# One step of a convolution / latent attention backbone: a new order for the opening, a layer norm in parts, masks built later

## The chip, the core and the metric

The kernel runs on one core of one Trainium2 chip. The core has a matrix engine (TensorE, PE in the rows), a vector engine (VectorE, DVE), a scalar engine (ScalarE, ACT), a general one (GpSimd, POOL) and SyncE (SP), which here only issues transfers. Each has its own strictly ordered queue; they meet in semaphores. The metric is the time of one execution on the device in microseconds. Everything is float32. Where a product must be exact and fast, each operand is kept as a high and a low part (`fp32r`), and three matmuls, high x high, high x low and low x high, make one product (`mm3`). Some products are left as plain f32 matmuls; each of these is two records in the trace.

## The reference, cut to what matters

```python
def adaln(cond, w, b):
    m = jax.nn.silu(cond) @ w + b                    # w: 1024 x 6144
    return jnp.split(m[:, None, :], N_MOD, axis=-1)  # shift1, scale1, gate1, shift2, scale2, gate2

hp = modulate(rms_norm(xp, norm1_g[i]), mp[0], mp[1])   # 128 context tokens
hs = modulate(rms_norm(xs, norm1_g[i]), ms[0], ms[1])   # 256 latent tokens

def conv_module(h, pw1, dw, dw_b, ln_g, ln_b, pw2):
    a, g = jnp.split(h @ pw1, 2, axis=-1)            # pw1: 1024 x 2048
    u = a * jax.nn.sigmoid(g)
    u = depthwise_conv(u, dw, width=31) + dw_b
    u = jax.nn.silu(layer_norm(u, ln_g, ln_b))
    return u @ pw2
```

Layer 0 is this module and a dense SwiGLU, layer 1 latent attention and a mixture of eight experts, of which each token takes two. There are two condition vectors (`c` and `c_ctx`), so the modulation product has two rows.

## The kernel before

Weights come in chunks of 1 MB (128 partitions x 2048 floats) into a ring `raw` of six slots. SyncE's queue is one written list of `load` calls: slot s is loaded when chunk s - 6 has been used (modulation) or split into its two parts (all else). `make_hi` (ScalarE, 1.9 us) and `make_lo` (VectorE, 2.3 us) split a chunk into `wh` and `wl`, rings of three.

Opening (layer 0). Chunks 0 to 7 are `ada_w`, columns 0 to 2047 (shift and scale), 128 input channels each; x comes after the third. `ada` multiplies one: four matmuls of 512 columns, column block j to PSUM partitions 32j and up:

```python
for j in range(4):
    last = pe.matmul(ps[32 * j:32 * j + 32, ADA_BANKS[q][0], :], cst[:, k, :], raw[:, s % RAW, j * 512:(j + 1) * 512], ...)
```

All eight have to be in before `add_bias`, `turn_rows` (transposes) and `modulation` give shift and scale for each channel. `norm_act` then modulates the eight transposed blocks of 128 channels, `split_block` splits them, and eight rounds r of the first projection follow: chunk `PW1 + 3r` holds 256 output channels for all 1024 input channels, 48 matmuls of 384 tokens each, and after them two modulation chunks of group 1 (`ada`). After each second round comes the sigmoid (`sig`), and `glu(t)` writes `u`. VectorE puts the taps of six of the eight channel blocks between its other work (`add_taps`, `ROUND_TAPS`, `POST_TAPS`). TensorE does the last two blocks as 62 matmuls with diagonal matrices, which ScalarE makes, with twelve modulation chunks between them.

Layer norm. The column sums and squares are summed on TensorE over all partitions; one square root and one reciprocal over all 399 columns, then eight blocks: scale (VectorE), SiLU (ScalarE), split (VectorE), and `pw2_block` for each.

Experts (layer 1). The first tile's rows are gathered by a matmul while six indirect transfers of GpSimd scatter all rows to `xs_dram`. After them GpSimd builds the masks `selL` of the last tile with some twenty small operations. In TensorE's list its three transposes and three narrow matmuls (`last_tile`) stand after the second chunk of the first tile's second weight. SyncE waits for the scatters before it loads `xrow` and the next tile's chunks.

## Time and profile before

| what | value |
|---|---|
| time, median of 3 runs | 1447.17 us (1446.88 to 1450.38) |
| the profiled execution's own time | 1447.64 us |
| its span | 1445.9 us |
| TensorE busy | 1369.8 us (95%) |
| VectorE busy | 1060.7 us (73%) |
| ScalarE busy | 756.3 us (52%) |
| GpSimd busy | 100.6 us (7%) |
| HBM traffic | 242 GB/s over the span |

Busy times overlap, so they don't add up to the span. The clock of TensorE has two levels, 1.2 and 2.4 GHz; a view shows it as the granted share, 0.50 or 1.00. A record's length includes the way through the array, so records that follow each other closely are longer than the distance between their starts.

### The profile page before, as it was taken

Reading aid. Unit: us, or ns where it says so; the run is one execution under the profiler, and the core shown is the slowest. Engines: PE = TensorE matmul, PEld = TensorE weight load, DVE = VectorE, ACT = ScalarE, POOL = GpSimd, SP = SyncE. Lnnn points to the kernel's source line nnn. Section 1 sums busy time; section 2 is a strip of 40 time slices with the busy share of each in tenths; the row PEclk is TensorE's granted clock in tenths of the full one; section 3 lists DMA queues with packets and bytes.
Section 4 is the critical chain, followed back from the end, with each engine's and each line's share of the span. In section 5 each row is a group of like instructions: output and inputs, shape, how many; then the busy total and the mean of one; then the engine's idle time right before and its main releaser. Section 6 shows DMA issues by size and latency. Waiting matters only on the chain.

```text
span 1445.9 us, 18716 instructions
## 1 busy us (share of the span) xinstructions
PE 1369.8 (95%) x6687; PEld 1100.4 (76%) x6687; DVE 1060.7 (73%) x1328; ACT 756.3 (52%) x764; POOL 100.6 (7%) x129
## 2 busy tenths in 40 slices
PE   4999989999999989899999978799999999999997
PEld 1885456999999978677777757587878878878875
DVE  1689985443433457888888889588888888888986
ACT  2431355222312255655555545577777777777773
POOL 2000000401000001100000015200000000000003
PEclk8999999999999989999999998899999999999999
DMA  9898556989743324322222235799999999999994
GB/s 376 293 339 322 204 203 225 400 337 64 198 145 103 122 50 128 104 66 66 79 80 87 89 116 206 301 375 375 363 385 380 364 363 395 369 362 381 385 361 152
DMA packets 91914, 351.17 MB, mean 243 GB/s; under 512 B 7279, under 2 KB 43447, under 8 KB 62679
## 3 DMA queue, kind: packets, MB, share of 16 engines
q1 hardware_dynamic: 81088, 316.95, 61.4%
q0 software_dynamic: 9040, 28.66, 5.8%
q10 hardware_dynamic: 1735, 4.89, 0.8%
q8 instruction: 30, 0.49, 0.1%
q14 instruction: 21, 0.17, 0.0%
HBM read 326.13 MB, written 24.35 MB: 242 GB/s over the span
## 4 chain that ended last, share of the span: by engine, by line
PE 81%; DVE 8%; ACT 3%; issue 3%; POOL 2%; DMA 1%; ACTq 0%; DVEq 0%
PE ps L277 23%; PE ps L279 22%; PE ps L278 22%; PE ps L1699 3%; PE ps L1644 3%; DVE wl L261 2%; DVE hm L1551 2%; PE ps L1945 2%; DMA raw<-in_conv_pw 1%; PE ps L1976 1%; ACT wh L255 1%; PE ps L1949 1%; POOL xs_dram L660 1%; PE ps L2107 1%; ACT QB L850 0%
## 5 line engine op out<-in xcount | busy, mean ns | idle before, releaser
L261 DVE TENSOR_TENSOR wl<-raw,wh 128x2048 fp32r<-128x2048 f32 x253 | 575.9, 2290 | 151.8 <-ACT wh L255 151.6
L255 ACT ACTIVATE wh<-raw 128x2048 fp32r<-128x2048 f32 x253 | 484.1, 1917 | 306.0 <-PE ps L279 267.4
L277 PE MATMUL ps<-wh,xgh 128*128 128x512 f32 x432 | 173.5, 402 | 0.1
L279 PE MATMUL ps<-wh,xgl 128*128 128x512 f32 x432 | 171.1, 396 | 0.0
L278 PE MATMUL ps<-wl,xgh 128*128 128x512 f32 x432 | 171.0, 396 | 0.0
L277 PE MATMUL ps<-hTh,wh 128*128 128x384 f32 x480 | 164.7, 343 | 1.8 <-DVE hTl L417 1.8
L278 PE MATMUL ps<-hTl,wh 128*128 128x384 f32 x480 | 163.3, 340 | 0.0
L279 PE MATMUL ps<-hTh,wl 128*128 128x384 f32 x480 | 163.0, 340 | 0.0
L277 PE MATMUL ps<-wh,hgh 128*128 128x512 f32 x288 | 118.2, 410 | 3.6 <-DVE hgl L1557 1.9
L278 PE MATMUL ps<-wl,hgh 128*128 128x512 f32 x288 | 115.8, 402 | 0.0
L279 PE MATMUL ps<-wh,hgl 128*128 128x512 f32 x288 | 115.6, 402 | 0.0
L1072 DVE SCALAR_TENSOR_TENSOR v<-u,dwT,v 128x399 f32<-128x399 f32 x180 | 99.1, 639 | 0.0
L277 PEld LDWEIGHTS ps<-hTh,wh 128*128 128x128 f32 x480 | 90.5, 189 | 10.8 <-issue 7.9
L1158 DVE TENSOR_TENSOR ff<-ps,fs 128x384 f32<-128x384 f32 x22 | 12.3, 558 | 114.9 <-PE ps L279 114.9
L279 PEld LDWEIGHTS ps<-wh,xgl 128*128 128x128 f32 x432 | 81.4, 188 | 19.8
L277 PEld LDWEIGHTS ps<-wh,xgh 128*128 128x128 f32 x432 | 81.4, 188 | 19.1 <-DVE wl L261 0.4
L278 PEld LDWEIGHTS ps<-wl,xgh 128*128 128x128 f32 x432 | 81.4, 188 | 18.3
L278 PEld LDWEIGHTS ps<-hTl,wh 128*128 128x128 f32 x480 | 90.7, 189 | 0.4
L279 PEld LDWEIGHTS ps<-hTh,wl 128*128 128x128 f32 x480 | 90.6, 189 | 0.0
L277 PEld LDWEIGHTS ps<-wh,hgh 128*128 128x128 f32 x288 | 55.2, 192 | 20.8 <-DVE wl L261 5.5
L279 PEld LDWEIGHTS ps<-wh,hgl 128*128 128x128 f32 x288 | 55.3, 192 | 13.6
L278 PEld LDWEIGHTS ps<-wl,hgh 128*128 128x128 f32 x288 | 55.4, 192 | 12.5
(368 smaller groups left out, 2122.7 us busy)
## 6 DMA issues: line engine op xcount, KB each, us to landing
raw<-in_moe_w SPq DMA_DIRECT2D x180, 1024.0 KB, 6.1
raw<-in_ada_w SPq DMA_DIRECT2D x48, 1024.0 KB, 6.6
raw<-in_ffn_w SPq DMA_DIRECT2D x33, 1024.0 KB, 11.5
raw<-in_conv_pw SPq DMA_DIRECT2D x12, 1024.0 KB, 9.2
raw<-in_mla_wo SPq DMA_DIRECT2D x8, 1024.0 KB, 4.8
xs_dram<-hf POOLq DMA_DIRECT2D x14, 512.0 KB, 21.2
ys_dram<-hf POOLq DMA_DIRECT2D x14, 512.0 KB, 22.3
raw<-in_mla_wuq SPq DMA_DIRECT2D x8, 768.0 KB, 4.6
```

The costliest lines, as they stand in the source:

```text
L255: act.activation(wh[:, split_no(s) % HL, :], raw[:, s % RAW, :], ACT.Copy).then_inc(hi_made, 1)
L261: eng.tensor_tensor(wl[:, split_no(s) % HL, :], raw[:, s % RAW, :], wh[:, split_no(s) % HL, :], ALU.subtract).then_inc(lo_made, 1)
L277: nc.tensor.matmul(out_, sh, mh, start=start, stop=False)
L278: nc.tensor.matmul(out_, sh, ml, start=False, stop=False)
L279: return nc.tensor.matmul(out_, sl, mh, start=False, stop=stop)
L660: pool.indirect_dma_start(out=xs_dram[:, :], out_offset=bass.IndirectOffsetOnAxis(ap=rows_of[:, c, i:i + 1], axis=0), in_=xn[:, c, :], in_ ...
L1072: dve.scalar_tensor_tensor(out=v[:, j, :], in0=u[:, j, w:w + CV], scalar=dwT[:, w * DK + j:w * DK + j + 1], in1=v[:, j, :], op0=ALU.mult, ...
L1551: dve.tensor_tensor(hm[:, g, :].rearrange("p (j r) -> p r j", j=4), ps[:, 3 + g, :].rearrange("p (r j) -> p r j", j=4), ms[:, g, :].rearra ...
L1644: last = pe.matmul(ps[32 * j:32 * j + 32, ADA_BANKS[q][0], :], cst[:, k, :], raw[:, s % RAW, j * 512:(j + 1) * 512], start=k == 0, stop=k ...
L1699: pe.matmul(ps[:, i, 0:CV], diag[:, m % DIAGS, :], u[:, DVE_BLOCKS + i, w:w + CV], start=w == 0, stop=w == CW - 1).then_inc(sem("diag_used ...
L1945: pe.matmul(ps[:, 2 * h + c // 2, a:b], QB[:, h, c * P:(c + 1) * P], KT[:, h, k0:k1], start=True, stop=False)
L1949: last = pe.matmul(ps[:, 2 * h + c // 2, a:b], QB[r0:r1, 2, c * P:(c + 1) * P], KR[r0:r1, k0:k1], start=False, stop=True)
```

## The change

- Opening: `ada_w` and the first half of `conv_pw1`'s columns come in other chunks. A modulation chunk holds the shift and scale columns of two channel blocks (2 x 256) for four of the eight input blocks, so two chunks (`OPEN`) give a pair p of channel blocks its modulation. Each chunk is two transfers of 512 KB. x is first in the queue. `ada_pair(p)` sums eight matmuls of 512 columns into PSUM partitions 32p to 32p + 31. Each pair has its own bias, transposes and modulation.
- The first two rounds of the projection become one pass: `open_block(k)` adds input block k to four output blocks (12 matmuls), between the pairs. Rounds 2 to 7 stay, with the sixteen chunks of group 1 as `ADA_ROUND` says.
- The taps in the rounds are 78 instead of 74 (`ROUND_TAPS`); `u` is cleared by GpSimd after the bias loads; VectorE clears `ar`.
- Layer norm: root and reciprocal in three parts (`LN_PARTS`), the first block scaled, passed through SiLU, split and waited for in these parts.
- Masks: TensorE's, ScalarE's and VectorE's steps of `last_tile` move from the first expert's tile into the static tile behind it.
- Semaphores are merged (`first_turned` into `x_turned`, `weights_made` into `tab_ready`), and the counts shift.

```diff
     ADA_G = DK
-    PW1 = ADA_G
-    ADA1 = PW1 + 3 * DK
+    QUARTERS = DK // 2
+    PAIR_BLOCKS = 4
+    OPEN = (0, 1, 3, 4, 5, 6, 8, 9)
+    ADA_ROUND = (0, 0, 3, 3, 3, 3, 2, 2)
+    PW1 = [2, 7] + [10 + r - 2 + sum(ADA_ROUND[:r]) for r in range(2, DK)]
+    ADA1 = 4 * ADA_G
     GATE1 = ADA1 + ADA_G
     PW2 = GATE1 + ADA_G
     GATE2 = PW2 + DK // 2 + 2
...
-    ROUND_TAPS = (0, 0, 13, 13, 12, 12, 12, 12)
+    ROUND_TAPS = (0, 0, 14, 14, 13, 13, 12, 12)
     POST_TAPS = (24, 30, 38)
     GATE_EARLY = 4
+    LN_PARTS = ((0, P, 0), (P, SV + P, P), (SV + P, CV, 2 * P))
     TILE_CH = 6 * NG
     NEXT = MOE + 12
...
+        def landed(s):
+
+            return 16 * (s // RAW + 1 + sum(o % RAW == s % RAW for o in range(min(s + 1, PW1[2]))))
 
...
-                make_hi(act, PW1)
-            act.wait_ge(sem("mods"), 8 * layer + 4 * n + 4)
             for j in blocks:
+                if j in (0, 4):
+                    make_hi(act, PW1[j // 4])
+                act.wait_ge(sem("mods"), 4 * (j // 2 + 1))
                 act.wait_ge(*of_norm(q, "turned", DK, j + 1))
                 for cond, a, b in ((1, 0, P), (0, P, T)):
...
-            for n in range(ADA_G):
-                if n == 3:
-                    sp.dma_start(x[:, 0, :], d["x_prompt"][0]).then_inc(sem("x_in"), 16)
-                    sp.dma_start(x[:, 1:3, :], d["x_sample"][0].rearrange("(c p) n -> p c n", p=P)).then_inc(sem("x_in"), 16)
-                load_ada(n, 0, n)
-            for r in range(DK):
-                load(sp, PW1 + 3 * r, rows(d["conv_pw1"][0], 0, DK, r % 2 * D + r // 2 * 256, 256), as_rows(256, DK))
-                for i in range(2):
-                    load_ada(PW1 + 3 * r + 1 + i, 0, ADA_G + 2 * r + i)
+            def load_pair(s, w, half, c0):
+
+                for t in range(2):
+                    load(sp, s, rows(w, 4 * half, 4, t * D + c0, 256),
+                         lambda slot: slot.rearrange("p (k t n) -> p k t n", k=4, t=2)[:, :, t, :])
+
+            sp.dma_start(x[:, 0, :], d["x_prompt"][0]).then_inc(sem("x_in"), 16)
+            sp.dma_start(x[:, 1:3, :], d["x_sample"][0].rearrange("(c p) n -> p c n", p=P)).then_inc(sem("x_in"), 16)
+            for p in range(QUARTERS):
+                for half in range(2):
+                    load_pair(OPEN[2 * p + half], d["ada_w"][0, :, 0:CH], half, 256 * p)
+                if p % 2 == 0:
+                    load_pair(PW1[p // 2], d["conv_pw1"][0], p // 2, 0)
+            n = ADA_G
+            for r in range(2, DK):
+                load(sp, PW1[r], rows(d["conv_pw1"][0], 0, DK, r % 2 * D + r // 2 * 256, 256), as_rows(256, DK))
+                for i in range(ADA_ROUND[r]):
+                    load_ada(PW1[r] + 1 + i, 0, n)
+                    n += 1
+
             def load_pw2(q):
                 load(sp, pw2_chunk(q), rows(d["conv_pw2"][0], 2 * q, 2, 0, D), as_rows(D, 2))
...
-            fetch_bias(0)
+            b = d["ada_b"][0, 0:CH].rearrange("(t q n) -> q t n", t=2, q=QUARTERS)
+            for p in range(QUARTERS):
+                pool.dma_start(ab[32 * p:32 * p + 2, 0, :].rearrange("p (t n) -> p t n", t=2),
+                               b[p].partition_broadcast(2)).then_inc(sem("bias_in0"), 16)
+            fetch_bias(0, 1)
+            pool.memset(u[:, :, :], 0.0).then_inc(sem("zeroed"), 1)
...
-            for r in range(DK):
+            for r in range(1, DK):
                 if r + 1 < DK:
-                    make_hi(act, PW1 + 3 * (r + 1))
-                for n in range(3 * r, 3 * r + 3):
-                    diagonal(n)
+                    make_hi(act, PW1[r + 1])
+                if r >= 2:
+                    for n in range(4 * (r - 2), 4 * (r - 1)):
+                        diagonal(n)
                 if r % 2 == 1:
                     t = r // 2
-                    act.wait_ge(chunk_used, used(PW1 + 3 * r))
+                    act.wait_ge(chunk_used, used(PW1[r]))
...
-            act.activation(sd, ps[:, 5, 0:CV], ACT.Sqrt, scale=1.0 / D, bias=epsc[:, 0:1]).then_inc(sem("ln_root"), 1)
-            for j in range(DK):
-                act.wait_ge(sem("ln_scaled"), j + 1)
+            for a, b, _ in LN_PARTS:
+                act.activation(sd[:, a:b], ps[:, 5, a:b], ACT.Sqrt, scale=1.0 / D, bias=epsc[:, 0:1]).then_inc(sem("ln_root"), 1)
+            for i, (_, b, o) in enumerate(LN_PARTS):
+                act.wait_ge(sem("ln_scaled"), i + 1)
+                act.activation(hf[:, 0, o:o + P], v[:, 0, b - P:b], ACT.Silu, scale=vT[:, LNG:LNG + 1],
+                               bias=vT[:, LNB:LNB + 1]).then_inc(sem("ln_done"), 1)
+            for j in range(1, DK):
+                act.wait_ge(sem("ln_scaled"), TC + j)
                 for a, b, o in ((0, P, 0), (P, T, SV - P)):
                     act.activation(hf[:, j, a:b], v[:, j, a + o:b + o], ACT.Silu, scale=vT[:, LNG + j:LNG + j + 1],
...
                 make_hi(act, MOE + k + 3)
-                if k == UP + 1:
-                    act.wait_ge(sem("last_tile"), TC + 1)
-                    for c in range(TC):
-                        act.activation(sel[:, c, :], ident[:, :], ACT.Copy, scale=rt[:, 9, c, 3:4])
...
+                    if static and k == UP + 2:
+                        act.wait_ge(sem("last_tile"), TC + 1)
+                        for c in range(TC):
+                            act.activation(sel[:, c, :], ident[:, :], ACT.Copy, scale=rt[:, 9, c, 3:4])
+                        act.activation(selT[:, :], ps[:, 6, 0:T], ACT.Copy).then_inc(sem("last_tile"), 1)
...
+            def add_bias_pair(p):
+
+                dve.wait_ge(ada_used, 2 * (p + 1))
+                if p == 0:
+                    dve.wait_ge(sem("bias_in0"), 64)
+                else:
+                    dve.wait_ge(sem("rows_turned"), p - 1)
+                own = slice(32 * p, 32 * p + 32)
+                dve.tensor_tensor(ar[own, p % 2, :], ps[own, p % 2, :], ab[own, 0, :], ALU.add).then_inc(sem("rows_added"), 1)
+
+            def modulation_pair(p):
+
+                dve.wait_ge(sem("rows_turned"), p + 1)
+                t = ps[:, p % 2, :].rearrange("p (i c) -> p c i", i=4)
+                two = slice(2 * p, 2 * p + 2)
+                for cond in range(2):
+                    dve.tensor_copy(modv[:, 0, cond, 0, two], t[:, 32 * p + cond, 0:2]).then_inc(sem("mods"), 1)
+                    dve.scalar_tensor_tensor(out=modA[:, 0, 0, cond, two], in0=t[:, 32 * p + cond, 2:4], scalar=1.0,
+                                             in1=vT[:, N1G + 2 * p:N1G + 2 * p + 2],
+                                             op0=ALU.add, op1=ALU.mult).then_inc(sem("mods"), 1)
+
             taps = sem("dve_taps")
...
+            step(dve.memset(ar[:, :, :], 0.0))
             norm_dve(dve, step, "conv")
             dve.wait_ge(sem("vec_turned"), 1)
             dve.tensor_copy(dwT[:, 0:P], ps[:, 7, P:2 * P]).then_inc(sem("dw_made"), 1)
             dve.tensor_copy(dwT[:, P:CW * DK], ps[:, 7, 2 * P:P + CW * DK]).then_inc(sem("dw_made"), 1)
             dve.tensor_copy(vT[:, :], ps[:, 7, 0:64]).then_inc(sem("dw_made"), 1)
             dve.wait_ge(sem("dw_made"), 3)
-            add_bias(0)
-            modulation(0)
-            split_block(dve, "conv", "conv_modulated", 2, 0)
-            make_lo(dve, PW1)
-            for j in range(1, DK):
-                split_block(dve, "conv", "conv_modulated", 2, j)
+            add_bias_pair(0)
+            modulation_pair(0)
+            for p in range(QUARTERS):
+                if p % 2 == 0:
+                    make_lo(dve, PW1[p // 2])
+                split_block(dve, "conv", "conv_modulated", 2, 2 * p)
+                if p + 1 < QUARTERS:
+                    add_bias_pair(p + 1)
+                split_block(dve, "conv", "conv_modulated", 2, 2 * p + 1)
+                if p + 1 < QUARTERS:
+                    modulation_pair(p + 1)
             dve.wait_ge(sem("zeroed"), 3)
             dve.wait_ge(sem("dw_made"), 2)
             done = 0
-            for r in range(DK):
-                if r % 2 == 0 and r > 0:
+            for r in range(1, DK):
+                if r % 2 == 0:
                     glu(r // 2 - 1)
                 if r + 1 < DK:
-                    make_lo(dve, PW1 + 3 * (r + 1))
-                if r == 4:
+                    make_lo(dve, PW1[r + 1])
+                if r == 5:
                     add_bias(1)
-                if r == 5:
+                if r == 6:
                     modulation(1)
                 add_taps(done, done + ROUND_TAPS[r])
...
             dve.wait_ge(sem("ln_centred"), DK)
-            for j in range(DK + 2):
+            for i in range(TC + 1):
+                if i < TC:
+                    a, b, _ = LN_PARTS[i]
+                    dve.wait_ge(sem("ln_root"), i + 1)
+                    step(dve.reciprocal(rs[:, a:b], sd[:, a:b]))
+                if i > 0:
+                    o = LN_PARTS[i - 1][2]
+                    dve.wait_ge(sem("ln_done"), i)
+                    high = dve.tensor_copy(hTh[:, 0, o:o + P], hf[:, 0, o:o + P])
+                    if i < TC:
+                        step(high)
+                    else:
+                        high.then_inc(sem("h_hi"), 1)
+                        dve.wait_ge(sem("h_hi"), SPLITS.index("ln") * DK + 1)
+                    dve.tensor_tensor(hTl[:, 0, o:o + P], hf[:, 0, o:o + P], hTh[:, 0, o:o + P], ALU.subtract)\
+                        .then_inc(sem("ln_h_lo"), 1)
+                if i < TC:
+                    dve.tensor_tensor(v[:, 0, a:b], v[:, 0, a:b], rs[:, a:b], ALU.mult).then_inc(sem("ln_scaled"), 1)
+            for j in range(1, DK + 2):
                 if j < DK:
                     dve.tensor_tensor(v[:, j, :], v[:, j, :], rs, ALU.mult).then_inc(sem("ln_scaled"), 1)
-                if j >= 2:
-                    split_block(dve, "ln", "ln_done", 2, j - 2)
+                if j >= 3:
+                    split_block(dve, "ln", "ln_done", 2, j - 2, 1)
             add_bias(4)
             make_lo(dve, pw2_chunk(2))
...
-                ada(n, 0, n)
-                if n == 5:
-                    turn_vectors()
-                if n == 6:
-                    pe.wait_ge(sem("dw_made"), 3)
-                    norm_pe(pe, "conv", CONV_BANKS, range(6))
-            turn_rows(0)
-            norm_pe(pe, "conv", CONV_BANKS, range(6, DK))
-            for r in range(DK):
-                t, s = r // 2, PW1 + 3 * r
+            def ada_pair(p):
+
+                for half in range(2):
+                    s = OPEN[2 * p + half]
+                    pe.wait_ge(raw_in[s % RAW], landed(s))
+                    for k in range(4):
+                        last = pe.matmul(ps[32 * p:32 * p + 32, p % 2, :], cst[:, 4 * half + k, :],
+                                         raw[:, s % RAW, k * 512:(k + 1) * 512],
+                                         start=half == k == 0, stop=half == 1 and k == 3)
+                    last.then_inc(ada_used, 1)
+
+            def turn_pair(p):
+
+                pe.wait_ge(sem("rows_added"), p + 1)
+                for i in range(4):
+                    last = pe.transpose(ps[:, p % 2, i * P:(i + 1) * P], ar[:, p % 2, i * P:(i + 1) * P], ident[:, :])
+                last.then_inc(sem("rows_turned"), 1)
+
+            def open_block(k):
+
+                pe.wait_ge(sem("conv_h_lo"), k + 1)
+                hi, lo = parts(PW1[k // 4], 512, 4)
+                for m in range(PAIR_BLOCKS):
+                    last = mm3(ps[:, 2 + m, 0:T], hi[:, k % 4, m * P:(m + 1) * P], lo[:, k % 4, m * P:(m + 1) * P],
+                               hTh[:, k, :], hTl[:, k, :], k == 0, k == DK - 1)
+                if k % 4 == 3:
+                    last.then_inc(chunk_used, 1)
+
+            pe.wait_ge(sem("cst_made"), 1)
+            turn_vectors()
+            ada_pair(0)
+            pe.wait_ge(sem("dw_made"), 3)
+            norm_pe(pe, "conv", CONV_BANKS, (0, 1))
+            turn_pair(0)
+            for p in range(QUARTERS):
+                if p + 1 < QUARTERS:
+                    ada_pair(p + 1)
+                    norm_pe(pe, "conv", CONV_BANKS, (2 * p + 2, 2 * p + 3))
+                if p % 2 == 0:
+                    wait_parts(pe, PW1[p // 2])
+                open_block(2 * p)
+                if p + 1 < QUARTERS:
+                    turn_pair(p + 1)
+                open_block(2 * p + 1)
+            n_ada = ADA_G
+            for r in range(2, DK):
+                t, s = r // 2, PW1[r]
                 wait_parts(pe, s)
                 hi, lo = parts(s, 256, DK)
                 if r % 2 == 0 and t >= 2:
...
                 if r % 2 == 1 and t >= 1:
                     pe.wait_ge(sem("sig_made"), t)
                 for n in range(2 * DK):
-                    m, k = (n % 2, n // 2) if r == 0 else (n // DK, n % DK)
+                    m, k = n // DK, n % DK
                     b = m + (4 if r % 2 else 2 - 2 * (t % 2))
-                    if r == 0:
-                        pe.wait_ge(sem("conv_h_lo"), max(k, m) + 1)
                     last = mm3(ps[:, b, 0:T], hi[:, k, m * P:(m + 1) * P], lo[:, k, m * P:(m + 1) * P],
                                hTh[:, k, :], hTl[:, k, :], k == 0, k == DK - 1)
                 last.then_inc(chunk_used, 1)
-                for i in range(2):
-                    ada(s + 1 + i, 0, ADA_G + 2 * r + i)
-                if r == 4:
+                for i in range(ADA_ROUND[r]):
+                    ada(s + 1 + i, 0, n_ada)
+                    n_ada += 1
+                if r == 5:
                     turn_rows(1)
...
-                pe.wait_ge(sem("ln_h_lo"), k + 1)
+                pe.wait_ge(sem("ln_h_lo"), c + 1 if k == 0 else TC + k)
                 for h in range(2):
                     last = mm3(ps[:, 2 * c + h, :], hTh[:, k, c * P:(c + 1) * P], hTl[:, k, c * P:(c + 1) * P],
                                hi[:, i, h * 512:(h + 1) * 512], lo[:, i, h * 512:(h + 1) * 512],
...
-                if i == 1:
-                    pe.wait_ge(sem("last_tile"), TC)
-                    for c in range(TC):
-                        pe.transpose(ps[:, 6, c * P:(c + 1) * P], selL[:, c, :], ident[:, :])
-                    for c in range(TC):
-                        last = pe.matmul(ps[:, 7, 0:2], selL[:, c, :], GL[:, c, :], start=c == 0, stop=c == TC - 1)
-                    last.then_inc(sem("last_tile"), 1)
...
+                    if static and i == 1:
+                        pe.wait_ge(sem("last_tile"), TC)
+                        for c in range(TC):
+                            pe.transpose(ps[:, 6, c * P:(c + 1) * P], selL[:, c, :], ident[:, :])
+                        for c in range(TC):
+                            last = pe.matmul(ps[:, 7, 0:2], selL[:, c, :], GL[:, c, :], start=c == 0, stop=c == TC - 1)
+                        last.then_inc(sem("last_tile"), 1)
```

## Rows read from the trace of the kernel before

**Rows 1.** The page, part 4: the chain that ended last, by engine.
```profile
PE 81%; DVE 8%; ACT 3%; issue 3%; POOL 2%; DMA 1%; ACTq 0%; DVEq 0%
```

**Rows 2.** The chain in order of time: start us, us, what.
```profile
37.48 0.55 PE ps L277
...
47.76 1.85 PE ps L1644 x16
...
60.14 0.37 PE ps L277
...
121.88 0.82 ACT sg L732
...
123.80 2.28 PE ps L1699 x6
```

**Rows 3.** Windows, modulation matmuls only (L1644): us, PE busy (records), weight loads.
```profile
47.72:48.10 0.38, 0.38 (x4) 0.13 (x8) 1.00 0.00 0
48.10:48.20 0.10, 0.10 (x8) 0.05 (x4) 1.00 0.00 0
```

**Rows 4.** Timeline and source of L2164, f32 matmuls over the whole array.
```profile
1431.04 3.60 PE L2164 MATMUL ps<-yacc,sel 128*128 128x512 f32 x8
...
L2164 PE MATMUL ps<-yacc,sel x12: 592/592/593, 1431.0 to 1437.6; 128*128 128x512 f32 x12
```

**Rows 5.** Windows, all engines: us, busy by engine, PEclk, DMA share, GB/s.
```profile
22.00:24.00 2.00, 1.45 (x10) 0.20 (x8) 1.20 (x2) 0.88 (x1) 0.00 (x0) 0.50 1.02 426
28.00:30.00 2.00, 2.00 (x22) 1.83 (x24) 0.00 (x0) 0.00 (x0) 0.00 (x0) 1.00 1.10 350
```

**Rows 6.** Timelines of ACT, DVE and PE, then DMA issues, opening.
```profile
5.64 0.46 ACTq L706 DMA_DIRECT2D vec<-in_conv_dw  x1
...
33.20 6.54 ACT L321 ACTIVATE hf<-ps,modv,modA 128x128 f32<-128x128 f32 x16
...
35.01 2.29 DVE L261 TENSOR_TENSOR wl<-raw,wh 128x2048 fp32r<-128x2048 f32 x1
...
27.77 2.18 PE L396 MATMUL ps<-ident,xn 128*128 128x128 f32 x18
...
ab<-in_ada_b POOLq DMA_DIRECT2D x8, 12.0 KB, 6.0
```

**Rows 7.** Timeline of DVE, taps of the convolution.
```profile
95.27 6.62 DVE L1072 SCALAR_TENSOR_TENSOR v<-u,dwT,v 128x399 f32<-128x399 f32 x12
```

**Rows 8.** The chain in order of time, layer norm.
```profile
195.48 0.60 ACT sg L749
196.11 2.66 DVE sg L1130
...
200.42 0.37 DVE hTh L415
200.82 0.57 DVE hTl L417
201.52 0.77 PE ps L277
```

**Rows 9.** Timelines of PE and SP, chain and xrow's tile, experts.
```profile
913.77 0.90 PE L2119 MATMUL ps<-ident,selL 128*128 128x128 f32 x3 [8.96 <-POOL selL L678]
...
930.57 0.39 PE L277 MATMUL ps<-wh,xgh 128*128 128x512 f32 x1
...
907.71 0.33 SPq L521 DMA_DIRECT2D xrow<-xs_dram  x1
...
915.74 0.63 PE ps L277
...
921.50 0.39 PE ps L278
...
929.79 0.24 PE ps L279
...
DMA to landing us min/median/max: 3.5/3.5/3.5
```

More of the change, by code:

```diff
@@ L204, in hybrid_conv_mla_diffusion_step @@
         ada_used, chunk_used = sem("ada_used"), sem("chunk_used")
-        kinds = [False] * ADA_G + [True, False, False] * DK + [False] * (2 * ADA_G) + [True] * 6 + [False] * DK
+        kinds = [n in PW1 for n in range(ADA1)] + [False] * (2 * ADA_G) + [True] * 6 + [False] * DK
         splits = [s for s, k in enumerate(kinds) if k]
@@ L252, in make_hi @@
             turns = None if loop is None else (loop[0], loop[1] // RAW * 16)
-            act.wait_ge(raw_in[s % RAW], at(16 * (s // RAW + 1), turns))
+            act.wait_ge(raw_in[s % RAW], at(landed(s), turns))
             free_parts(act, s, loop)
@@ L343, in norm_act_rows @@
                 between()
-            act.wait_ge(sem("mods"), 8 * layer + 4 * n + 4)
+            act.wait_ge(sem("mods"), 8 * layer + 4 * n + 4 * QUARTERS)
             for j in range(DK):
@@ L410, in split_dve, with split_block @@
                 split_block(dve, q, made, per, j)
-        def split_block(dve, q, made, per, j):
-            dve.wait_ge(sem(made), per * (j + 1))
+        def split_block(dve, q, made, per, j, more=0):
+            dve.wait_ge(sem(made), per * (j + 1) + more)
             dve.tensor_copy(hTh[:, j, :], hf[:, j, :]).then_inc(sem("h_hi"), 1)
@@ L548, in _, with fetch_bias @@
             pool.memset(ab[:, :, :], 0.0).then_inc(sem("zeroed"), 1)
-            pool.memset(u[:, :, :], 0.0).then_inc(sem("zeroed"), 1)
-            def fetch_bias(layer):
+            def fetch_bias(layer, g0):
                 b = d["ada_b"][layer].rearrange("(g j n) -> j g n", g=3, j=4)
                 for j in range(4):
-                    pool.dma_start(ab[32 * j:32 * j + 2, :, :], b[j].partition_broadcast(2)).then_inc(sem(f"bias_in{layer}"), 16)
+                    pool.dma_start(ab[32 * j:32 * j + 2, g0:3, :], b[j, g0:3].partition_broadcast(2)).then_inc(sem("bias_in1"), 16)
             def keep_gate(layer, which):
                 q = 3 * layer + 1 + which
-                pool.wait_ge(sem("rows_added"), q + 1)
+                pool.wait_ge(sem("rows_added"), q + QUARTERS)
                 for i in range(2):
@@ L1514, in weights @@
                 step(dve.tensor_scalar(gap[:, :, 2:3], gap[:, :, 1:2], 1.0, None, ALU.add))
-                dve.reciprocal(gap[:, :, 3:4], gap[:, :, 2:3]).then_inc(sem("weights_made"), 1)
+                dve.reciprocal(gap[:, :, 3:4], gap[:, :, 2:3]).then_inc(sem("tab_ready"), 1)
             has, to, w = xj[:, 0, :, :], xj[:, 1, :, :], xj[:, 2, :, :]
@@ L1586, in tile @@
                         hidden_lo(k - 1, L3)
+                    if static and k == UP + 2:
+                        dve.wait_ge(sem("last_tile"), TC + 1)
+                        step(dve.tensor_copy(slot_w[:, :], ps[:, 7, 0:2]))
+                        dve.wait_ge(sem("last_tile"), TC + 2)
+                        dve.sem_inc(sem("y_copied"), 1)
                     if k == 2 * UP:
@@ L1653, in turn_rows @@
                 last.then_inc(sem("rows_turned"), 1)
-            for n in range(ADA_G):
-                ada(n, 0, n)
-                if n == 5:
-                    turn_vectors()
-                if n == 6:
-                    pe.wait_ge(sem("dw_made"), 3)
-                    norm_pe(pe, "conv", CONV_BANKS, range(6))
-            turn_rows(0)
-            norm_pe(pe, "conv", CONV_BANKS, range(6, DK))
-            for r in range(DK):
-                t, s = r // 2, PW1 + 3 * r
+            def ada_pair(p):
+                for half in range(2):
+                    s = OPEN[2 * p + half]
+                    pe.wait_ge(raw_in[s % RAW], landed(s))
+                    for k in range(4):
[3 more added lines that the diff above has]
+                    last.then_inc(ada_used, 1)
@@ L2006, in _ @@
                 last = pe.transpose(ps[:, 3, c * P:(c + 1) * P], krh[:, c, :, :].rearrange("p a b -> p (a b)"), ident[:, :])
-            last.then_inc(sem("first_turned"), 1)
+            last.then_inc(sem("x_turned"), 1)
             pe.wait_ge(sem("q_copied"), 1)
```

46 lines of the change are left out of this document (17 added, 29 removed).

## The prediction

> **What bounds the kernel now.** The page first. TensorE holds 81% of the chain that ended last [rows 1], so the time is TensorE's work plus the places where it stands or runs at the lower clock. The chain in order of time and the timelines show three such places that the change touches.
>
> The opening: the first projection matmul runs at 37.48, round 2 of the projection begins at 60.14, the last round ends at 121.88, and the convolution on TensorE begins at 123.80 [rows 2]. Up to 37 the loads set the pace (DMA moves 350 to 426 GB/s all the time [rows 5]), after it TensorE does.
>
> The layer norm: from the square root at 195.48 to the first second-projection matmul at 201.52 TensorE stands, and its first matmuls take 0.43 [rows 8].
>
> The experts' first tile: TensorE stands 8.96 us for masks that GpSimd finishes at 913.7, and then runs 0.43 matmuls until 921.5, where the usual one is 0.24 [rows 9]. The expert stage is TensorE's everywhere else, so what is saved here is not given back.
>
> **The opening, step by step.** Before, the four matmuls of a modulation chunk (`ada`) write partitions 0, 32, 64 and 96. The windows show that they run side by side: four records in the first 0.4 us, the next four start beside their ends at 48.1 to 48.2, some 0.46 later, and a chunk (8 records, two for each matmul) costs 0.93, half of the 1.85 for two [rows 2, 3]. After, all eight matmuls of a pair accumulate into one strip of 32 partitions, so no two can be side by side. The nearest rows for one strip: 0.46 between successive records of the same strip [rows 3], and 0.43 for 512-wide f32 records that follow each other in the whole array, (3.60 - 0.59) / 7 with 0.592 for one [rows 4]. I take 0.43, the row of the same order of work. Then 8 chunks x 8 records x 0.43 = 27.5 us, where they cost 8 x 0.93 = 7.4. This is the main cost, and the change's text doesn't show it. Above, weight loads that are no longer hidden would add up to 64 x 0.11 = 7.
>
> Transfers don't set the pace then. A chunk in runs of 1 KB moves at 350 GB/s (28 to 30, a projection chunk), one in 8 KB runs at 426 [rows 5], so 3.0 us each instead of 2.5; a pair is 6 to 9 us of transfer and 6.9 of matmuls plus 4.2 of blocks.
>
> The Trainium skill (DMA: Bandwidth & Descriptors, Specifications) says that transfers from 512 B on reach line rate. The trace disagrees at 1 KB, 350 against 426; by the rule the chunks would land 5 us sooner in sum, and the forecast would not move, as TensorE is behind.
>
> Start: x and the first chunk are 2.6 MB, and from about 2 us at 0.42 MB/us, with 1.4 from last byte to landing and 0.5 more for the short runs, that is 10.5. The vectors' last load is issued at 5.64 and small loads take 6.0 [rows 6], so their transposes end near 11.7. I take 11.7 (10.5 to 13). TensorE comes from idling, so it starts at the 1.2 GHz level. In the experts the rise came 5.8 us into dense work (921.5 after 915.7) [rows 9], and the phase can be luckier or not; I take 5, of which half is lost, 2.5 (1.3 to 3.6).
>
> TensorE's queue is strict, so the sum is: 11.7 + 27.5 + 2.5; 96 projection matmuls at 0.177, 17.0 (a round of 48 and 1.85 of packed modulation take 10.5, from 47.76 + 1.85 to 60.14, with 0.2 of changing over [rows 2]); 40 transposes, 24 of the norm and 16 of the rows, at 0.12, 4.8 (18 in 2.18 [rows 6]); 14 changes of operand at 0.1, 1.4. End: 64.9. The last pair's blocks go: modulation, four ScalarE pieces of 0.41, two splits of 0.95 [rows 8], then ScalarE (which must wait for all eight splits) 1.9 and VectorE 2.29 for the next chunk's two parts [rows 6]. That is ready 1.1 after the last block. Round 2 starts at 66.0 instead of 60.14: **+5.9** (from 0 to +17).
>
> Rounds 2 to 7 hold 14 modulation chunks before the last projection chunk's end, where the old ones held 10: 4 x 0.93, **+3.7**. All 16 come packed, as before.
>
> VectorE: 78 taps instead of 74 before glu(3), at 0.545 [rows 7], in a stretch that is only 3.7 longer, and after short waits for the projection chunks of rounds 4 and 6, which are loaded only when the preceding round's modulation slots come free. Summed piece by piece from 65.9 (five low parts of 2.2, three glu of 0.9, 42.5 of taps, 0.7 of bias and modulation, 11 waiting) it reaches glu(3) at 133.8 or so, while its sigmoid is ready near 132.3. **+1.5** (0 to 4). The convolution's four fewer taps are worth nothing: TensorE's 62 diagonals and the sums end last, VectorE's taps 1.2 earlier.
>
> At nothing: x loaded first (norms 8 us earlier, no one waits for them); the memset of u behind the bias loads (glu needs it 50 us later); one memset of ar (VectorE idle till 8); two loads for a chunk (0.4 us of SP each, 1.5 of transfer); semaphores merged. If the cover of the bias loads were gone, pair 0 would wait 1 to 2 us.
>
> **Layer norm in parts.** Before: 195.48 root, 196.11 reciprocal 2.65, scale, SiLU, a split of 0.37 and 0.57, first matmul 201.52 [rows 8]. After: a third's root 0.3, reciprocal 0.85, scale 0.25; ScalarE has to do three roots and the 1.28 table load before the first SiLU, which gives 197.7 and 198.1; split 0.6. First matmul 198.8, the other thirds ready at 200.6 and 201.7. At 0.43 each the six matmuls of a third take 2.6, so none waits; the rise comes 3.4 after the start, as before. Block 1 needs VectorE until 204.1, and the 18 matmuls of block 0 end at 204.5 instead of 207.3. **-2.8** (-1.5 to -3.5).
>
> **Masks later.** Without the stop, four expert chunks of 12 x 0.235 = 2.8 follow at 904.8. The row transposes among them need xrow, issued at 907.71 after the scatters and landed 3.5 later [rows 9], so they run at 911.2 (0.8 of waiting). The chunks end at 917.7. The next tile's first chunk is issued behind xrow at 908.13, lands near 913.5, its halves are ready at 917.7, the rows' low part at 918.9: tile 0 begins at 919.0, before 930.57 [rows 9]. -11.5, and 1.4 for three transposes and six narrow matmuls in the static tile. ScalarE's 1.45 and VectorE's 0.16 there lie in a slack of 0.9 a chunk with two chunks in hand. **-10.1** (-8 to -12.2).
>
> Sum: 5.9 + 3.7 + 1.5 - 2.8 - 10.1 = -1.8. The profiled execution took 1447.64 with a span of 1445.9; 1447.64 - 1.8 = 1445.8, and the median 1447.17 lies 0.5 lower: **1445.4**.
>
> TensorE: Matmul & The Clock Gate, in the Trainium skill (Measured speedup vs the span model), gives 3.07 for four tiles at once, not 4. By it a lone strip's chunk would cost 0.93 x 3.07 = 2.86, eight 22.8, and the time would be 1440.8, faster. The rows give 3.7 (0.43 x 8 / 0.93), and no run here has the lone strip.
>
> **Rivals.**
> A, the clock stays low. No row shows a long run of matmuls in one strip. Packed ones with gaps of 0.5 ran 18 to 24 at 1.2 GHz without a rise (22 to 24: busy 1.45 of 2.00, granted 0.50) [rows 5]. If lone strips don't raise it, the 64 records cost 27.5 more, about half of the 96 block matmuls 0.144 more each (0.43 x 384 / 512 = 0.32 against 0.177), 7, less the 2.5 and 1.5 counted: +30, **1476**. Against it: TensorE is never idle here. 24%.
> B, the pace is the transfers', and the matmuls of one strip overlap. Then the last modulation chunk lands at 38.4 (8.4 for x, ten of 3.0), behind it 0.9, 0.7, four blocks of 2.1 and 0.5 for a turn: end 49.3, round 2 at 50.7, -9.4; with 3.7, 1.5 and -12.9 that is -17, **1430**. Against it: rows 3 and 4 agree on 0.43 to 0.46. 12%, with all else that makes the opening short.
> C, weight loads of the one strip show between the records: +7, **1452.5**, slower. It decides from 0.07 a record on. For it: each record is followed by another load for the same 32 columns; against: in rows 3 the loads lie under the matmuls. 11%.
> D, the mask's stop comes back as a wait for the first chunks of tile 0, which SP issues only after the scatters: gain 4 instead of 10, **1451.5**. For it: xrow goes out only at 907.71 [rows 9], when TensorE has 10 us of chunks left, and everything of tile 0 is queued behind it. 7%.
>
> **Chances.** Forecast 46%, own range 1440 to 1451. A change of 0.3% (4.3 us) is about what can be told from none: below 1442.8 lie B and a quarter of the forecast's, 24%; above 1451.5 A, most of C and half of D, 41%; between 35%. The range 1436 to 1478 leaves out most of B and a part of A.
>
> **What would show it.** Modulation matmuls in the opening as records 0.43 apart, one pair 6.9 at 2.4 GHz, granted clock 1.00 from 20 on (A: 0.50 with 0.86 apart; B: pairs follow their landing). Round 2 near 66, convolution's start near 135. The first matmul of the second projection 3.3 after the square root's start, instead of 6.0. No POOL releaser before the masks' transposes, tile 0 some 11 earlier relative to the start of the expert chunks. I am wrong if round 2 starts before 60 or after 75.

## The result: 0.5% slower, and the profile after

The kernel after takes 1454.2 us (median of 8 runs, 1452.29 to 1463.27), the kernel before 1447.07 in the runs beside it: a ratio of 1.0052, 95% interval 1.0034 to 1.0071, so by the ratio 7.5 us slower (5 to 10). The profiled execution took 1453.96 with a span of 1452.2, 6.3 longer than the span of before. The forecast was 1445.4, faster by 1.8: the measured time lies outside its own range of 1440 to 1451, inside the wide one of 1436 to 1478, on the other side of before, and 8.8 us off.

The chain by engine, from the page (it answers to [rows 1]): TensorE has lost share to VectorE, and GpSimd's part, the masks, is gone.

```profile
PE 76%; DVE 11%; ACT 4%; issue 3%; DMA 1%; POOL 0%; DVEq 0%; ACTq 0%; POOLq 0%
```

The same landmarks in both traces say where. Each row is a stretch of TensorE's work (us, before and after), and beside it stands what was forecast.

| stretch | before | after | difference | forecast |
|---|---|---|---|---|
| start to round 2's first matmul | 60.14 | 66.94 | +6.8 | +5.9 |
| round 2 to the convolution's first matmul | 63.66 | 71.05 | +7.4 | +5.2 |
| convolution to the square root | 71.68 | 73.14 | +1.5 | 0 |
| square root to the first second-projection matmul | 6.04 | 3.51 | -2.5 | -2.8 with the next row |
| from there to the six modulation chunks behind the projection | 36.25 | 39.36 | +3.1 | |
| from there to the experts' gathering matmuls | 635.06 | 636.51 | +1.5 | 0 |
| gathering matmuls to the end | 573.07 | 561.69 | -11.4 | -10.1 |

**Opening.** TensorE's timeline of the kernel after, two of the four pairs. The answer to [rows 3, 4]: 16 records of one strip follow each other 0.43 apart, (7.05 - 0.59) / 15, never side by side, and the first pair, at the start, is 2.6 longer.

```profile
12.85 9.64 PE L1731 MATMUL ps<-raw,cst 128*32 128x512 f32 x16
23.91 7.05 PE L1731 MATMUL ps<-raw,cst 128*32 128x512 f32 x16
```

**Rounds.** First VectorE's timeline: it has done its taps at 78.5 and then idles 8.25 for a projection chunk's high part, with the taps of the next round queued behind it. Then the chain in order of time (start, us, what), which answers to [rows 2].

```profile
71.84 6.63 DVE L1122 SCALAR_TENSOR_TENSOR v<-u,dwT,v 128x399 f32<-128x399 f32 x12
86.73 2.29 DVE L270 TENSOR_TENSOR wl<-raw,wh 128x2048 fp32r<-128x2048 f32 x1 [8.25 <-ACT wh L264]
```
```profile
66.94 0.45 PE ps L286
...
87.06 1.90 PE ps L1714 x16
88.97 9.26 DMA raw<-in_conv_pw
98.26 1.92 ACT wh L264
100.20 2.30 DVE wl L270
102.55 0.45 PE ps L286
...
136.38 0.62 DVE v L1122
137.00 0.94 DVE u L1130 x2
137.99 2.36 PE ps L1804 x3
```

Read it from the DMA line: the projection chunk of round 5 is issued when a modulation matmul of round 3 frees its slot (88.97), lands 9.3 later, needs 1.9 and 2.3 for its parts, and TensorE, which is through with round 4, waits 1.4 for it. At the end VectorE's taps and its last sigmoid product set the convolution's start (TensorE's timeline):

```profile
133.52 1.92 PE L1714 MATMUL ps<-raw,cst 128*32 128x512 f32 x16
137.99 2.36 PE L1804 MATMUL ps<-u,diag 128*128 128x399 f32 x3 [2.55 <-DVE u L1130]
```

The transfers had not been the limit before: the DMA share was 0.52 and 0.14 while that slot was still in use. Windows (us, busy by engine, PEclk, DMA share, GB/s).

```profile
66.00:72.00 6.00, 5.22 (x30) 5.06 (x30) 5.07 (x7) 3.78 (x6) 0.00 (x0) 1.00 0.52 178
72.00:78.00 6.00, 6.00 (x45) 4.04 (x43) 6.00 (x12) 0.00 (x0) 0.00 (x0) 1.00 0.14 20
```

The convolution then begins at the lower clock, 0.50 granted, behind a wait of 2.5. Three matmuls in 2 us, where [rows 2] have six in 2.28.

```profile
138.00:140.00 2.00, 2.00 (x3) 1.16 (x4) 2.00 (x4) 0.27 (x1) 1.18 (x3) 0.50 0.99 418
```

**Layer norm.** TensorE's timeline, the lines with idle time. The first line is 3.51 behind the square root (211.13); in [rows 8] it is 6.04. The third is what the forecast lacks: the row transposes of the fifth modulation part wait 3.25 for the bias addition, which VectorE does behind all its splits (its own timeline, the line below).

```profile
214.64 0.47 PE L286 MATMUL ps<-wh,hTh 128*128 128x512 f32 x1 [1.11 <-DVE hTl L1200]
220.04 0.50 PE L286 MATMUL ps<-wh,hTh 128*128 128x512 f32 x1 [0.76 <-DVE hTl L426]
227.75 0.66 PE L1722 MATMUL ps<-ident,ar 128*128 128x128 f32 x4 [3.25 <-DVE ar L1071]
```
```profile
227.01 0.68 DVE L1071 TENSOR_TENSOR ar<-ps,ab 128x512 f32<-128x512 f32 x1
```

The same two instructions in the timelines of the kernel before, with no idle time ahead of the transposes: VectorE's addition 14.28 behind the root (195.48), TensorE's transposes 16.09 behind it.

```profile
209.76 0.68 DVE L1042 TENSOR_TENSOR ar<-ps,ab 128x512 f32<-128x512 f32 x1
```
```profile
211.57 0.60 PE L1652 MATMUL ps<-ident,ar 128*128 128x128 f32 x4
```

**Experts.** TensorE's timeline: row transposes, tile 0's first matmul, the masks' transposes in the static tile. None has an idle time before it, where [rows 9] have 8.96. From the gathering matmuls to tile 0's first matmul it is 45.71, before 57.74: -12.0.

```profile
929.73 1.04 PE L2205 MATMUL ps<-ident,xrow 128*128 128x128 f32 x8
...
936.22 0.40 PE L286 MATMUL ps<-wh,xgh 128*128 128x512 f32 x1
...
960.39 0.49 PE L2238 MATMUL ps<-ident,selL 128*128 128x128 f32 x3
```

### The profile page after: what moved, and what is told of

The parts are those of the page before. It is cut to its first block, busy times and chain, and to the rows that moved or that the text cites. A ratio compares the mean times of both kernels' runs of the same rounds, so it can differ in the third digit from the quotient of the medians.

```text
span 1452.2 us, 18812 instructions
## 1 busy us (share of the span) xinstructions
PE 1385.6 (95%) x6698; PEld 1103.8 (76%) x6699; DVE 1065.2 (73%) x1352; ACT 756.3 (52%) x767; POOL 106.0 (7%) x133
## 4 chain that ended last, share of the span: by engine, by line
PE 76%; DVE 11%; ACT 4%; issue 3%; DMA 1%; POOL 0%; DVEq 0%; ACTq 0%; POOLq 0%
PE ps L286 21%; PE ps L288 21%; PE ps L287 21%; PE ps L1804 3%; DVE wl L270 2%; PE ps L1714 2%; DVE hm L1623 2%; PE ps L2050 2%; ACT wh L264 1%; DVE v L1122 1%; PE ps L2081 1%; PE ps L2054 1%; PE ps L2212 1%; DMA raw<-in_conv_pw 1%; PE ps L2171 1%
## 5 line engine op out<-in xcount | busy, mean ns | idle before, releaser
L288 PEld LDWEIGHTS ps<-wh,hgl 128*128 128x128 f32 x288 | 54.2, 188 | 13.1
## 6 DMA issues: line engine op xcount, KB each, us to landing
raw<-in_ffn_w SPq DMA_DIRECT2D x33, 1024.0 KB, 11.1
```

What stands on the lines that cost most here:

```text
L288: return nc.tensor.matmul(out_, sl, mh, start=False, stop=stop)
```

## Experiments

The theory after the traces: the three parts add up; the opening costs TensorE's lone strip, then the late chunks of the rounds; the norm's gain is eaten by the transposes behind it. Times are medians; ratios are to the kernel before run beside it, with their 95% intervals. A landmark is from the profiled run.

### The parts alone

**e1_masks_only**: before, with this alone (the same move on ScalarE and VectorE).

```diff
             for i in range(UP):
                 up_chunk(MOE + UP, i, 3, hgh, hgl, None)
-                if i == 1:
-                    ...
                     up_chunk(NEXT + UP, i, 3, xgh, xgl, L)
+                    if static and i == 1:
+                        ...
```

> The kernel before with only the masks' transposes moved into the static tile. My theory: the stop for GpSimd's masks (8.96) and the low clock behind it go, three transposes and six narrow matmuls come back: -10 us against before (-9 to -11). Rival: the change's gain there needs the rest of the change, or is given back by a wait for the first chunks of the tile: -4 or less. Subtracting the two traces at fixed points gives -9.9 in the whole change, so near -9.9 here if the parts add up.

1437.41 us, ratio 0.9922 (0.9909 to 0.9935), 11.1 under the kernel before and at the far end of what was expected. From the gathering matmuls to the end 561.8, in the whole change 561.7. The gain is all there without the rest, and nothing takes it back.

**e2_norm_only**: before, with the layer norm of the kernel after: `LN_PARTS` on ScalarE and VectorE, and on TensorE `pe.wait_ge(sem("ln_h_lo"), c + 1 if k == 0 else TC + k)`.

> The kernel before with only the layer norm in parts. Theory A (from the trace after): the first second-projection matmul comes 2.5 us sooner behind the square root, but the row transposes behind the first chunk then wait about 3.3 for VectorE's bias addition, which stands behind the thirds' extra instructions: in sum +0.6 us (0 to +1). Rival B (my forecast): -2.8. Rival C: the loss seen in the whole change came from the opening (another phase of the clock), and alone this part gains 2 or more.

1451.75 us (1448.70 to 1459.01), ratio 1.002 (1.0003 to 1.0038): slower, A, and by more than A said; the trace is of a run of 1448.77, near the lowest, and accounts for the +1.9 that follows, not for the rest. First matmul 3.51 behind the square root, but the modulation chunks behind the projection start at 239.72 instead of 237.77, +1.9. Timeline and a window of TensorE's wait:

```profile
212.15 1.11 PE L1674 MATMUL ps<-ident,ar 128*128 128x128 f32 x4 [3.25 <-DVE ar L1048]
```
```profile
212.00:214.00 2.00, 1.85 (x7) 1.66 (x8) 2.00 (x2) 1.53 (x1) 1.08 (x2) 0.50 0.03 6
```

The wait is the same 3.25, and here the clock is at 0.50 behind it. In the profiled run of the kernel after it stayed at 1.00, which is why that one shows +0.6 for the norm and this one +1.9. In e4, e5, e6 and e10 below the same wait is there and the four transposes take 1.0 to 1.1, nearly as here: of six traces with this wait only that of the kernel after has them at 0.66.

**e9_opening_only**: the kernel after with the masks and the norm as before.

> The kernel before with the new opening alone; the masks and the layer norm are as before. Theory A (the three parts add up): the convolution starts at 137.5 to 138 as in the kernel after, 14 later than before, and nothing of it is given back: 1447 + 14 + up to 1.5 of low clock = 1461 to 1463 us. Rival B: GpSimd's masks are independent of the opening, so that a later TensorE finds them ready and the stop of 8.96 swallows a part: 1456 or less.

1462.23 us, ratio 1.010 (1.0076 to 1.0125), in A's range. The convolution starts at 136.94, 13.1 later than before, and the gathering 13.7 later. The profiled run is the lowest of the four (1458.4) and ends 10.8 behind that of before, so that 2.9 comes back behind the gathering; the medians differ by 15. GpSimd's stop is 1.8 shorter and the gathering before it 1.7 longer. That is not B: e2, whose opening is the old one, has the same stop of 7.15, and the part on the masks below shows what the two traces share.

```profile
927.32 0.90 PE L2202 MATMUL ps<-ident,selL 128*128 128x128 f32 x3 [7.15 <-POOL selL L701]
```

The three alone make +14.5, +2.9 and -11.3, that is +6, known to some 5 us by their intervals; the whole change made +7.5 (5 to 10). So the parts add up within the noise.

### The opening: how many strips

**e5_four_strips** and **e6_two_strips**: after, with `STRIPS` 4 or 2.

```diff
-                        last = pe.matmul(ps[32 * p:32 * p + 32, p % 2, :], cst[:, 4 * half + k, :],
+                        g = (4 * half + k) % STRIPS
+                        last = pe.matmul(ps[32 * g:32 * g + 32, p % 2, :], cst[:, 4 * half + k, :],
 ...
-                    last = pe.transpose(ps[:, p % 2, i * P:(i + 1) * P], ar[:, p % 2, i * P:(i + 1) * P], ident[:, :])
+                    last = pe.matmul(ps[:, p % 2, 2 * i:2 * i + 2], ar[:, p % 2, i * P:(i + 1) * P], fold4[:, 0:2],
+                                     start=True, stop=True)
```

`fold4` holds ones at rows c, 32 + c, 64 + c and 96 + c of column c, so the narrow matmul turns the rows and adds the strips in one. Each pair's bias lies in rows 0 and 1 of zeroed space of its own (`sg`, and `ab` for the last).

> The kernel after, but the eight matmuls of a modulation pair go to four strips of 32 partitions in turn, the bias is added on all 128, and the row transposes become narrow matmuls that add the four strips up. Nothing else is changed. Theory A (the lone strip is the cost): the pair's 16 records take 1.9 instead of 7.05, TensorE's own work of the opening falls by 4 x 5.1 = 20, then the transfers set the pace, and round 2 starts at 50 to 52 instead of 66.9: -14 us against after (-10 to -16). Rival B (the order of loads and blocks costs, not the strip): round 2 starts after 60, -5 or less.

> The same with two strips instead of four. Theory A: two strips run side by side, a pair takes 3.5 instead of 7.05, so TensorE's work falls by 4 x 3.5 = 14, and round 2 starts near 53: -12 us against after (-9 to -14), between the kernel after and four strips. Rival B: only four strips overlap, two don't: 0 to -2.

Four: 1439.35 us, ratio 0.9951 (0.9927 to 0.9975). Two: 1442.82 us, ratio 0.9965 (0.9940 to 0.9989). They are 14.9 and 11.4 under the kernel after, as A expected; their intervals overlap, so the order of the two rests on the landmarks. A pair and round 2's first matmul in the timelines, four strips and then two:

```profile
33.28 1.92 PE L1743 MATMUL ps<-raw,cst 128*32 128x512 f32 x16
...
54.35 0.45 PE L293 MATMUL ps<-hTh,wh 128*128 128x384 f32 x1 [0.78 <-DVE wl L277]
```
```profile
31.20 3.63 PE L1743 MATMUL ps<-raw,cst 128*32 128x512 f32 x16
...
55.70 0.44 PE L293 MATMUL ps<-hTh,wh 128*128 128x384 f32 x1 [0.78 <-DVE wl L277]
```

Between e6 and e5 only the number of strips differs; against the kernel after the turning of the rows differs too. A pair goes 7.05, 3.63, 1.92, round 2 from 66.94 to 55.70 and 54.35. The lone strip is the cost, A. Its second half is wrong: round 2 didn't come at 50 to 52. With four strips TensorE waits only 3.3 for chunks (2.25 before 20.80 and 1.09 before 23.82), and its granted clock was 0.50 from 20 to 28, where two strips, with one wait of 1.10, had 1.00 (windows, four and two):

```profile
20.00:28.00 8.00, 6.11 (x26) 2.71 (x27) 4.36 (x6) 1.29 (x4) 0.00 (x0) 0.50 1.10 348
```
```profile
20.00:28.00 8.00, 6.90 (x39) 3.88 (x39) 4.89 (x10) 1.72 (x4) 0.00 (x0) 1.00 1.10 348
```

### The rounds

**e4_two_a_round**: after, with VectorE's bias addition and modulation and the row transposes one round later.

```diff
-    ADA_ROUND = (0, 0, 3, 3, 3, 3, 2, 2)
+    ADA_ROUND = (0, 0, 2, 2, 2, 2, 2, 6)
```

> The kernel after with two modulation chunks in each of rounds 2 to 6 and six behind round 7 (before it 3, 3, 3, 3, 2 and 2). A projection chunk then follows in the slot of an earlier projection chunk, which is free as soon as its two parts are made, instead of in one that a modulation matmul must free. Theory A: VectorE's idle time before low parts (8.25, 2.62 and 1.38 in the kernel after) goes, TensorE's wait of 1.4 before round 5 too; the convolution starts when TensorE is through its own work, 66.9 + 6 x 8.55 + 16 x 0.93 = 133.1 instead of 137.99, and at the full clock: -6 us against after (-4.5 to -6.5). Rival B: VectorE's taps alone are the bound (14 + 14 + 13 + 13 + 12 + 12), then the start stays at 136 or later: -2 or less.

1452.03 us, ratio 1.0033 (1.0013 to 1.0052), with a wide scatter (1448 to 1463); the profiled run's span is 5.3 under the one of after. A by the landmarks: the convolution starts at 133.42, the square root is at 205.12, 6.0 sooner. Of these 6.0 the rounds gave 4.1 (round 2 to the convolution 66.98 instead of 71.05) and the full clock in the convolution 1.4; 0.5 was there at round 2, ahead of this edit. VectorE's idle time before low parts falls from 15.2 to 6.2 (one of 3.28 is left, for round 6), TensorE's wait before round 5 is gone. The edit also puts four more modulation chunks between round 7 and the convolution, which would cover a late product; but VectorE reaches that product 9.6 sooner, which is the idle time saved and those 0.5, and now waits for the sigmoid. By the medians and ratios the gain is 2 to 3 and not 6, with scatter enough to hide the rest; the profiled run (1448.67) is near the lowest of the twelve.

**e10_fewer_taps**: after, with `ROUND_TAPS = (0, 0, 13, 13, 12, 12, 12, 12)`.

> The kernel after with VectorE's taps before the last sigmoid product as before the change: 13, 13, 12, 12, 12, 12 in rounds 2 to 7 (74 instead of 78), the other four behind it. Theory A (VectorE is late for the last product): it comes 4 x 0.545 = 2.2 sooner, TensorE's own work ends at 135.5, so the convolution starts at 135.8: -2.2 us against after. Rival B: the four taps come back at the end of VectorE's part of the convolution, where they have 1.2 us of room: -1 or less. Rival C: the projection chunk of round 5 is what is late for both engines, and VectorE idles as much longer: 0.

1453.52 us, ratio 1.0046 (1.0026 to 1.0067). The convolution starts at 135.55, 2.4 sooner (0.45 of it was there at round 2), near what A says, and the square root is at 208.86, 2.3 sooner, so the taps don't come back (against B). The last product is still late by 2.0 for TensorE. The median alone (-0.7) would not show it; in this profiled run the norm's wait ended at the lower clock as in e2.

### The norm's wait, and versions that are faster

**e3_turn_later**: after, with

```diff
-                if q == 0:
+                if q == 1:
                     turn_rows(4)
 ...
             make_lo(dve, pw2_chunk(2))
-            modulation(4)
             make_lo(dve, pw2_chunk(3))
+            modulation(4)
```

> The kernel after, with the row transposes of the fifth modulation part one second-projection chunk later on TensorE, and VectorE's modulation behind the next low part. Theory A: the wait of 3.3 us at the transposes goes, and nothing follows at once: -3.3 us against after (-2.5 to -3.5). Rival: TensorE then waits as long for the blocks or the next chunk's low part: 0 to -1.

1449.11 us, ratio 1.0013 (0.9997 to 1.0029). The transposes wait for nothing:

```profile
212.67 0.48 PE L286 MATMUL ps<-wh,hTh 128*128 128x512 f32 x1 [1.11 <-DVE hTl L1200]
218.05 0.50 PE L286 MATMUL ps<-wh,hTh 128*128 128x512 f32 x1 [0.75 <-DVE hTl L426]
230.80 0.60 PE L1722 MATMUL ps<-ident,ar 128*128 128x128 f32 x4
```

From the first of these matmuls to the modulation chunks it is 35.89, after 39.36: -3.5, A. The time fell by 5 us, more than A said. The rest in this trace is ahead of the edit: the convolution began 0.5 sooner and at the full clock (137.49 to 209.17, as long as before, 1.5 less than in the kernel after).

**e8_old_opening**: before, with the masks, the norm and this mending.

> The kernel before with the masks later, the layer norm in parts and the fifth part's row transposes one chunk later; the opening is the old one. If the parts add up: -10.4 (masks, measured) and -2.9 (the norm without its wait): span 1432.6 (1431 to 1435). Rival: the clock takes the norm's gain back: 1435 or more.

1435.61 us, ratio 0.9904 (0.9888 to 0.9921). Square root to modulation chunks 39.42 instead of 42.29, -2.9; at the end 2.4 under e1's span. The span of 1433.1 lies in the range that was expected.

**e7_all_mended**: after, with the edits of e3, e4 and e5.

> The kernel after with all three: four strips, two modulation chunks in a round, the fifth part's row transposes one chunk later. If the gains add up: 1454 - 14 - 6 - 5 = 1429 us (1424 to 1435), faster than before by over 1%. Rival: with the opening at the pace of the transfers, the projection chunks of the rounds come late, and VectorE's taps set the convolution's start: 1436 or more.

1429.56 us, ratio 0.9862 (0.9839 to 0.9885), at the sum of the gains. The convolution starts at 119.65, before at 123.80, and the square root to the modulation chunks takes 39.20. It is the fastest version: the idea of the change, with four strips at once.

## Why the forecast was wrong

**The opening: right in kind, near in size.** The lone strip, 27.5 us of matmuls, was the step that spoke against the change, and e5 and e6 show it. Pairs of 7.05 were forecast as 6.9. Start and low clock were forecast as 14.2 and measured as 12.85 plus 2.6. Round 2 came at 66.94 instead of 66.0, so close because the blocks, turns and last parts took 1.0 less than their terms.

The Trainium skill's figure (TensorE: Matmul & The Clock Gate, Measured speedup vs the span model), 3.07, stands there for four row tiles; for tiles in columns, as the strips here are, the same table has three tiles and 2.38. Carried over to four strips, as in the forecast's estimate, 3.07 would have given a faster kernel. The runs have 7.05 / 1.92 = 3.67 for four and 1.94 for two, so the measurement decides for the rows' 3.7.

**The rounds: VectorE's term too small, and a wait of TensorE left out.** +3.7 for four more modulation chunks and +1.5 for VectorE made 5.2; measured 7.4, and 1.5 of low clock behind it. The 3.7 is right: a chunk takes 0.93 in the rounds (2.78 for three). The step that failed is "after short waits for the projection chunks of rounds 4 and 6", with the 11 us of waiting that the sum gives VectorE. It idled 13.0 before low parts from round 2 on: 0.78, then 8.25, 2.62 and 1.38 for rounds 4, 5 and 6. One of these chunks was late for TensorE too (1.4 before round 5, a wait that the sum doesn't have), and the product came 2.5 late. The cause is the period of the loads. With one projection chunk in three, its slot of six was that of an earlier projection chunk, free once the parts are made; with one in four it is that of a modulation chunk of two rounds before, free only when TensorE has used it. e4 restores the old period, and the waits for rounds 4 to 6 fall to one of 3.28; e10 shows that fewer taps alone bring the start 2.0 nearer to round 2.

**The norm: the step sized right, the one behind it left out.** -2.8 was forecast, first matmul 3.3 after the root; 3.51 came, and e8 banks -2.9. What failed is that the sum stops at block 0 and block 1. The thirds cost VectorE eight more instructions in that stretch (12 for the first block instead of 4), its bias addition comes 15.88 behind the root instead of 14.28, and TensorE, which would be at the row transposes 13.4 behind the root instead of 16.1, has to wait for it there. Before, the addition was done 1.1 before TensorE came. The forecast never listed what TensorE has between the first chunk and the second. This is the largest miss: the stretch behind the first matmul, put at no change, is 3.1 longer in the profiled run and 4.4 in e2; e3 and e8 take the wait away and have the gain.

**The masks: right.** -11.5 + 1.4 forecast; -12.0 to tile 0 and +1.0 for the static tile measured, and rival D (the stop comes back as a wait for tile 0) did not happen. The -11.4 of the table compares two kinds of traces, though. In the traces of before, e5, e6 and e8 GpSimd takes 3.0 and 1.9 to issue the second and third transfer of the scatter, and `xrow` goes out 34.1 to 34.9 behind the gathering's first matmul; in the other eight it takes 1.0 for each, and `xrow` goes out 29.4 to 29.9 behind it, while the gathering's last 32 records take 5.4 to 5.6 instead of 3.8. Why a trace is of one kind or the other is open. Like with like, gathering to end, the masks gain 10.5 (573.1 in before, 562.6 in e8) and 9.5 (571.4 in e2, 561.8 in e1), where 10.1 was forecast. In e8 TensorE waits 1.05 for `xrow` (0.8 in the forecast) and 1.20 for the rows' low part, and tile 0 begins 46.5 behind the gathering's start (46.2). That TensorE waits for neither in the kernel after goes with its trace being of the other kind.

**Rivals.** A and C fell: from 17.97 on the records of the lone strip are 0.43 apart, with nothing between them. B fell for the lone strip. In the untouched stages between, after's trace is 1.5 longer; the 10 us behind the six modulation chunks (from 259.4 in after, from 243.2 in before) were granted 0.83 on the mean in after and 1.00 in before. Over the twelve traces that stretch, in which all these kernels are alike, takes from 634.9 to 640.6, so 1.5 is no more than the traces differ among themselves.

Two small slips in the forecast's sums change nothing in it: the start by x and the first chunk adds up to 10.1, not 10.5, and rival B's end of the opening to 48.9, not 49.3.

## What to carry to other kernels

- Four matmuls with few columns of output each are worth their four strips: when a layout asks that all go to one strip, spread the sum over the strips and let the matmul that turns the result add them up.
- When a step is made faster, list what the bound engine meets next in its queue, up to the next point where it has slack, and ask of each who delivers it and when. Here the first waiter moved 2.5 ahead and the second gave it back.
- In a ring of slots, what decides when a load can start is who used the slot before. Changing the order of two kinds of chunks changes that for all of them.

## What was not expected of the hardware

- f32 matmuls with 32 output partitions overlap nearly fully in two strips and in four: 16 records take 7.05, 3.63 and 1.92.
- At the start of the opening the granted clock reads 1.00, but the records of the one strip are 0.86 apart up to 17.97 and 0.43 from there, and are 1.06 long, as they are at a granted 0.50 in before (18 to 24), against 0.59 later. So here the spacing and length of equal records tell the clock, and the column doesn't. The first two in the timeline, and the window over them (modulation matmuls only):

```profile
12.85 1.06 PE L1731 MATMUL ps<-raw,cst 128*32 128x512 f32 x1
13.71 1.06 PE L1731 MATMUL ps<-raw,cst 128*32 128x512 f32 x1
```
```profile
14.00:15.00 1.00, 1.00 (x2) 0.18 (x1) 1.00 1.10 349
```

- The same wait of 3.25 ended at 1.00 in the kernel after and at 0.50 in e2, and the convolution began at 0.50 in after (137.99), at 1.00 in e3 (137.49), e9 (136.94) and e4 (133.42). One such phase is worth 1.3 to 1.8 us, as much as some of the terms that were to be told apart.
